# Gathering and turning the rows of two experts at once in a two-network fp32 kernel

## The reference, cut to what matters

```python
def expert_choice_moe(x, w_router, b_router, w_gate, w_up, w_down):
    b, s, d = x.shape
    cap = CAPACITY_FACTOR * s // N_EXPERTS            # 2 * 512 // 16 = 64 rows for each of 16 experts
    logits = jnp.einsum('bsd,de->bse', x, w_router).astype(jnp.float32) + b_router.astype(jnp.float32)
    aff = jax.nn.softmax(logits, axis=-1)
    gate, idx = lax.top_k(aff.transpose(0, 2, 1), cap)
    bidx = jnp.arange(b)[:, None, None]
    xs = x[bidx, idx]                                 # (b, 16, 64, 1024): the gather
    hid = jax.nn.silu(jnp.einsum('becd,edf->becf', xs, w_gate)) * jnp.einsum('becd,edf->becf', xs, w_up)
    ys = jnp.einsum('becf,efd->becd', hid, w_down) * gate[..., None].astype(x.dtype)
    return jnp.zeros_like(x).at[bidx, idx].add(ys)
```

## Time and profile before

| | |
|---|---|
| median of three runs | 2621.09 us |
| profiled execution, own time | 2624.85 us |
| its span, mean granted TensorE clock | 2622.9 us, 0.986 |
| TensorE busy (weight loads beside it) | 2505.8 us, 96% (1522.2 us) |
| VectorE, ScalarE, GpSimd busy | 1161.0, 476.1, 156.3 us |
| DMA, whole span | 601.78 MB, mean 229 GB/s |
| MoE stages | from about 1369 to 1840 us, and from about 2150 to the end |

### The profile page before, as it was taken

The page is one execution under the profiler, slowest core; times in us unless marked ns, Lnnn a source line. Parts: engine busy times, 40 slices in busy tenths (PEclk is TensorE's granted clock), DMA queues, the critical chain, the costliest instruction groups (busy, mean ns, idle before and its releaser), DMA issues.

```text
span 2622.9 us, 26789 instructions
## 1 busy us (share of the span) xinstructions
PE 2505.8 (96%) x10897; PEld 1522.2 (58%) x10897; DVE 1161.0 (44%) x2000; ACT 476.1 (18%) x1000; POOL 156.3 (6%) x265
## 2 busy tenths in 40 slices
PE   7999999999999999999999998889999999998898
PEld 4448888888888888556653333333556553333333
DVE  4774898655755644334641221112335641211112
ACT  2242121002222001234610000000224510000000
POOL 1140111000000000001200000000001000000000
PEclk9999999999999999999999999999999999999999
DMA  8642876451434225221259999999320359999998
GB/s 327 223 128 66 278 233 194 136 142 37 137 119 129 65 65 172 85 91 38 91 198 391 402 404 410 412 419 418 130 97 33 124 187 402 412 403 412 410 419 340
DMA packets 182794, 601.78 MB, mean 229 GB/s; under 512 B 9009, under 2 KB 123377, under 8 KB 157073
## 3 DMA queue, kind: packets, MB, share of 16 engines
q1 hardware_dynamic: 164544, 544.59, 54.7%
q0 software_dynamic: 16832, 51.22, 6.0%
q10 hardware_dynamic: 1296, 4.25, 0.4%
HBM read 593.74 MB, written 6.29 MB: 229 GB/s over the span
## 4 chain that ended last, share of the span: by engine, by line
PE 71%; DMA 18%; DVE 6%; ACT 1%; SPq 1%; issue 1%; another core or an unknown queue 0%; DVEq 0%; ACTq 0%
DMA arena<-in_w_down 17%; PE ps L2025 11%; PE ps L2583 7%; PE ps L2150 7%; PE ps L2613 6%; PE ps L2036 5%; PE ps L2262 5%; PE ps L2498 4%; PE ps L1996 3%; PE ps L2256 3%; PE ps L1945 2%; PE ps L2061 2%; PE ps L2276 2%; PE ps L2626 2%; PE ps L1920 1%; PE ps L2433 1%
## 5 line engine op out<-in xcount | busy, mean ns | idle before, releaser
L2583 PE MATMUL ps<-arena 128*64 128x512 f32 x2048 | 455.9, 599 | 20.3 <-DMA arena<-in_w_up 18.1
L2583 PEld LDWEIGHTS ps<-arena 128*64 128x64 f32 x2048 | 148.2, 138 | 311.8 <-issue 267.8
L2025 PE MATMUL ps<-arena 128*128 128x256 f32 x1280 | 277.9, 380 | 2.0 <-issue 2.0
L2025 PEld LDWEIGHTS ps<-arena 128*128 128x128 f32 x1280 | 242.9, 190 | 35.6 <-issue 3.4
L2613 PE MATMUL ps<-arena 128*64 128x512 f32 x896 | 211.1, 629 | 45.1 <-DMA arena<-in_w_down 43.7
L2150 PE MATMUL ps<-arena 128*128 128x256 f32 x896 | 193.8, 380 | 0.2 <-DVE arena L1453 0.2
L2150 PEld LDWEIGHTS ps<-arena 128*128 128x128 f32 x896 | 170.3, 190 | 23.4 <-issue 0.5
L2613 PEld LDWEIGHTS ps<-arena 128*64 128x64 f32 x896 | 72.3, 144 | 181.6 <-issue 179.9
L2036 PE MATMUL ps<-arena 128*128 128x256 f32 x672 | 146.3, 380 | 3.2 <-DVE arena L1266 1.7
L1804 DVE TENSOR_SCALAR arena<-ps,arena 128x512 f32<-128x512 f32 x32 | 22.7, 747 | 269.0 <-PE ps L2613 241.5
L2036 PEld LDWEIGHTS ps<-arena 128*128 128x128 f32 x672 | 127.6, 190 | 20.7 <-DVE arena L1274 2.0
(11 more groups left out here) (440 smaller groups left out, 3055.8 us busy)
## 6 DMA issues: line engine op xcount, KB each, us to landing
arena<-in_w_gate SPq DMA_DIRECT2D x64, 2048.0 KB, 49.1
arena<-in_w_up SPq DMA_DIRECT2D x64, 2048.0 KB, 41.9
arena<-in_w_down SPq DMA_DIRECT2D x56, 2048.0 KB, 41.7
arena<-in_ffn_w SPq DMA_DIRECT2D x24, 2048.0 KB, 9.8
arena<-in_w_mod POOLq DMA_DIRECT2D x80, 512.0 KB, 5.0
arena<-in_ffn_w SPq DMA_DIRECT2D x32, 1024.0 KB, 7.6
arena<-in_w_down SPq DMA_DIRECT2D x16, 1024.0 KB, 37.2
arena<-in_w_in SPq DMA_DIRECT2D x10, 1536.0 KB, 12.0
```

Source lines behind the costliest of these rows:

```text
L2025: ins = mm(ps[:, i % 6, 0:256], src[:, k, P * j:P * j + P], x[:, k, :], start=(k == 0), stop=(k == 3))
L2583: ins = mm(ps[CAP * half:CAP * half + CAP, bank, :], xsT[:, 4 * q + k, :], wv[:, k, 512 * half:512 * half + 512], start=(q == 0 and k == 0 ...
```

## The change

From the second pair of experts on, the rows of both experts come by one gather of 128 rows, over all 128 partitions. It is issued when the rows of the pair before are turned, in both rounds. The pair's rows are then turned in two rounds of four 128 x 128 transposes through PSUM bank 4; round 0 follows the products of the odd expert before, round 1 the first scatter behind it. TensorE's round 1 waits for VectorE's multiply of round 0. After even experts other than the first nothing is turned. Experts 0 and 1 are fetched and turned as before, except that VectorE's multiply is two operations of half the width. The turned rows of a pair take 1024 columns: `xsT` is now two tensors, one of them in the memory of the small tensors of the first block, which become parts of one tensor `first`. A copy of the index columns for pairs, `get_p`, is added on VectorE, and GpSimd waits for it.

```diff
--- before.py
+++ after.py
@@ -109,12 +109,13 @@
         ident, sel = const[:, C_ID:C_ID + P], const[0:8 * RPB_H, C_SEL:C_SEL + 8 * RPB_H]
         tbl = sb("tbl", [8 * RPB_H, 2, NA_HEADS, 40])
         ones = sb("ones", [P, P])
-        vrow = sb("vrow", [P, 2, P])
-        vA = sb("vA", [P, P])
-        vB = sb("vB", [P, B_ROWS])
+        first = sb("first", [P, 720])
+        vrow = first[:, 0:256].rearrange("p (i n) -> p i n", i=2)
+        vA = first[:, 256:384]
+        vB = first[:, 384:384 + B_ROWS]
         v2 = sb("v2", [P, DEPTH * VROWS])
-        modc = sb("modc", [P, 96])
-        small = sb("small", [P, 16, 8])
+        modc = first[:, 496:592]
+        small = first[:, 592:720].rearrange("p (i n) -> p i n", i=16)
         qkg = sb("qkg", [P, 2, DEPTH, QK])
         wr = sb("wr", [P, DEPTH, KC, EXPERTS])
         br = sb("br", [P, DEPTH, EXPERTS])
@@ -222,10 +223,13 @@
         get_i = at(38344, 16).bitcast(U32)
         idx_t = at(38360, 32, "p (i t) -> p i t", t=TC)
         iota = at(37952, P)
+        get_p = at(38392, 8).bitcast(U32)
         get_c = [sb(f"get_c{i}", [CAP, 1], U32) for i in range(2)]
+        get_pc = sb("get_pc", [P, 1], U32)
         oh = at(36928, 512)
-        xg = [at(38400, 1024)[CAP * i:CAP * i + CAP, :] for i in range(2)]
-        xsT = at(39424, 512, "p (k n) -> p k n", k=KC)
+        xg_pair = at(38400, 1024)
+        xg = [xg_pair[CAP * i:CAP * i + CAP, :] for i in range(2)]
+        xsT = [v.rearrange("p (k n) -> p k n", k=4) for v in (at(39424, 512), first[:, 0:512])]
         hid = at(39936, 512)
         hT2 = [at(lo, 512, "p (k n) -> p k n", k=4) for lo in (40448, 37440)]
         ye = [at(lo, 512) for lo in (40960, 49664)]
@@ -1757,6 +1761,7 @@
                 V.tensor_copy(get_i[0:CAP], idx_m).then_inc(sm["idx_cols"], 1)
                 dve.wait_ge(sm["top_ps"], 4 * l + 4)
                 V.tensor_copy(gate_t, ps[:, 6, 80:88])
+                V.tensor_copy(get_p, ps[:, 6, 88:96])
                 for t in range(TC):
                     ins = V.tensor_scalar(idx_t[:, :, t], ps[:, 6, 88:96], float(-P * t), None, add)
                 ins.then_inc(sm["idx_cols"], 1)
@@ -1765,8 +1770,16 @@
                 def gathered(e):
 
                     dve.wait_ge(sm["xst_ps"], 16 * l + e + 1)
-                    V.tensor_tensor(xsT, ps[:, 4, :].rearrange("p (k n) -> p k n", k=KC),
-                                    gperm[:, l, :].unsqueeze(2).to_broadcast([P, KC, CAP]), mul).then_inc(sm["xs_ready"], 1)
+                    for q in range(2):
+                        ins = V.tensor_tensor(xsT[q][:, :, CAP * e:CAP * e + CAP], ps[:, 4, 256 * q:256 * q + 256].rearrange("p (k n) -> p k n", k=4),
+                                              gperm[:, l, 4 * q:4 * q + 4].unsqueeze(2).to_broadcast([P, 4, CAP]), mul)
+                    ins.then_inc(sm["xs_ready"], 1)
+
+                def gathered_pair(i, q):
+
+                    dve.wait_ge(sm["xst_ps"], 16 * l + 2 * i + q + 1)
+                    V.tensor_tensor(xsT[q], ps[:, 4, :].rearrange("p (k n) -> p k n", k=4),
+                                    gperm[:, l, 4 * q:4 * q + 4].unsqueeze(2).to_broadcast([P, 4, P]), mul).then_inc(sm["xs_ready"], 1)
 
                 def scattered(i, t):
 
@@ -1785,10 +1798,15 @@
                     chain(V.scalar_tensor_tensor(hid, hid, 1.0, ps[:, 0, :], add, mul))
                     dve.wait_ge(*part_used(l, e, 3))
                     V.scalar_tensor_tensor(hid, hid, 0.5, ps[:, 1, :], mul, mul).then_inc(sm["hid_done"], 1)
-                    if e + 1 < EXPERTS:
-                        gathered(e + 1)
+                    if e == 0:
+                        gathered(1)
+                    elif par and e + 1 < EXPERTS:
+                        gathered_pair(i + 1, 0)
                     if i:
                         scattered(i - 1, 2 * par)
+                    if par and e + 1 < EXPERTS:
+                        gathered_pair(i + 1, 1)
+                    if i:
                         scattered(i - 1, 2 * par + 1)
                     if par == 0:
                         continue
@@ -2558,14 +2576,25 @@
 
                 def gathered(e):
 
-                    b = e % 2
-                    pe.wait_ge(got[b], 16 * (l * 8 + e // 2 + 1))
+                    pe.wait_ge(got[e], 16 * ((8 - 7 * e) * l + 1))
                     if e:
-                        pe.wait_ge(sm["ht_copied"], 16 * l + e - 1)
+                        pe.wait_ge(sm["ht_copied"], 16 * l)
                     for k in range(KC):
                         q, kk = divmod(k, 4)
-                        src = xg[b][:, 512 * q:512 * q + 512].rearrange("c (p k) -> c k p", k=4)[:, kk, :]
-                        ins = tr(ps[:, 4, CAP * k:CAP * k + CAP], src, ident[CAP * b:CAP * b + CAP, CAP * b:CAP * b + CAP])
+                        src = xg[e][:, 512 * q:512 * q + 512].rearrange("c (p k) -> c k p", k=4)[:, kk, :]
+                        ins = tr(ps[:, 4, CAP * k:CAP * k + CAP], src, ident[CAP * e:CAP * e + CAP, CAP * e:CAP * e + CAP])
+                    ins.then_inc(sm["xst_ps"], 1)
+
+                def gathered_pair(i, q):
+
+                    if q == 0:
+                        pe.wait_ge(got[0], 16 * (8 * l + i + 1))
+                        pe.wait_ge(sm["ht_copied"], 16 * l + 2 * i - 1)
+                    else:
+                        pe.wait_ge(sm["xs_ready"], 16 * l + 2 * i + 1)
+                    for kk in range(4):
+                        src = xg_pair[:, 512 * q:512 * q + 512].rearrange("c (p k) -> c k p", k=4)[:, kk, :]
+                        ins = tr(ps[:, 4, P * kk:P * kk + P], src, ident)
                     ins.then_inc(sm["xst_ps"], 1)
 
                 def piece(e, part):
@@ -2580,7 +2609,7 @@
                         wv, used = piece(e, part + q)
                         for k in range(4):
                             for half in range(2):
-                                ins = mm(ps[CAP * half:CAP * half + CAP, bank, :], xsT[:, 4 * q + k, :], wv[:, k, 512 * half:512 * half + 512],
+                                ins = mm(ps[CAP * half:CAP * half + CAP, bank, :], xsT[q][:, k, CAP * (e % 2):CAP * (e % 2) + CAP], wv[:, k, 512 * half:512 * half + 512],
                                          start=(q == 0 and k == 0), stop=(q == 1 and k == 3))
                         ins.then_inc(used, 1)
 
@@ -2629,21 +2658,25 @@
                 for e in range(EXPERTS):
                     i, par = divmod(e, 2)
                     n = 16 * l + e
-                    pe.wait_ge(sm["xs_ready"], n + 1)
+                    pe.wait_ge(sm["xs_ready"], 16 * l + (2 * i + 2 if i else e + 1))
                     inner(e, 0, 0)
                     if par == 0 and i:
                         pe.wait_ge(sm["ye_done"], 16 * l + 2 * i)
                     inner(e, 1, 2)
-                    if e + 1 < EXPERTS:
-                        gathered(e + 1)
+                    if e == 0:
+                        gathered(1)
+                    elif par and e + 1 < EXPERTS:
+                        gathered_pair(i + 1, 0)
                     if i:
                         pe.wait_ge(sm["oh_ready"], 8 * l + i)
                         scattered(i - 1, 2 * par)
                         if par == 0:
                             scattered(i - 1, 1)
+                    if par and e + 1 < EXPERTS:
+                        gathered_pair(i + 1, 1)
                     pe.wait_ge(sm["hid_done"], n + 1)
                     if e + 1 < EXPERTS:
-                        pe.wait_ge(sm["xs_ready"], n + 2)
+                        pe.wait_ge(sm["xs_ready"], 16 * l + (2 * (i + par) + 2 if e else 2))
                     for c in range(4):
                         ins = tr(ps[:, 4, P * c:P * c + P], hid.rearrange("p (n k) -> p k n", k=4)[:, c, :], ident)
                     ins.then_inc(sm["ht_ps"], 1)
@@ -2761,20 +2794,27 @@
 
                 def gather(e):
 
-                    b = e % 2
                     if e:
-                        G.tensor_copy(get_c[b][:, :], get_i[0:CAP, e:e + 1]).then_inc(sm["col_set"], 1)
-                        pool.wait_ge(sm["col_set"], 15 * l + e + 1)
-                    G.indirect_dma_start(out=xg[b], out_offset=None, in_=xn_dram,
-                                         in_offset=bass.IndirectOffsetOnAxis(ap=get_c[b][:, 0:1], axis=0)).then_inc(got[b], 16)
+                        G.tensor_copy(get_c[1][:, :], get_i[0:CAP, 1:2]).then_inc(sm["col_set"], 1)
+                        pool.wait_ge(sm["col_set"], 8 * l + 2)
+                    G.indirect_dma_start(out=xg[e], out_offset=None, in_=xn_dram,
+                                         in_offset=bass.IndirectOffsetOnAxis(ap=get_c[e][:, 0:1], axis=0)).then_inc(got[e], 16)
+
+                def gather_pair(i):
+
+                    G.tensor_copy(get_pc[:, :], get_p[:, i:i + 1]).then_inc(sm["col_set"], 1)
+                    pool.wait_ge(sm["col_set"], 8 * l + i + 2)
```

(9 more changed lines are left out.)

## The result

The changed kernel takes 2587.97 us (median of 4 runs, 2584.14 to 2589.86) against 2621.15 (2620.12 to 2622.59): 33.2 us less, ratio 0.987, 95% interval 0.986 to 0.988. The profiled execution took 2584.14 us with a span of 2582.3. The forecast was 2597 in 2586 to 2625, faster with 0.61.

A forecast was written before the change was run, and what follows sets the result against it. MoE stages were taken as bound by the weight DMA stream; dips -32.4 plus 7.0 left (-25.4), bytes +0.6 and head +0.3 gave -24.5: 2600.4 us profiled, 2597 as median, range 2586 to 2625.

The forecast's parts named there:

- The bound: MoE stages: from load 11 on, weight transfers set the end; TensorE work saved is worth nothing, DMA time itself.
- gather 2's bytes moved later: Layer 0: gather 2's rows, free before, now come inside the first pair gather in the full stretch, +0.6 us.
- The dips: MoE weight stream: the rate falls around each 64-row gather; 27 dips of 1.2 us, 32.4 us in the old kernel.
- What is left of a dip at full width: MoE weight stream: each 128-row pair gather still costs 0.5 us, 14 of them 7.0 us.
- head: Start of each MoE stage: two narrow multiplies behind gather 0 delay load 11 by 0.15 us, +0.3 over two layers.
- this very case: Landing in one half of the partitions causes the dips: 2597 us, own range 2588 to 2606, chance 0.52.
- the signs: Rate from 1400 to 1800 us rises from 411 to about 420 GB/s; each layer's stage ends about 12 us sooner.
- Turning: TensorE: even expert's gap -1.1 us, odd one's +1.3, per pair +0.2; no effect on the end.
- The doubtful place: First pair: buffers released at 1421.6 us, before loads under way run out at 1422.9; holds by little over 1 us.
- By rows: Rival for the MoE gathers: a dip's cost goes by rows, 2.4 us per 128-row gather; +2.1, 2623 us, chance 0.30.
- By transfer: Rival for the MoE gathers: each transfer costs one dip of 1.2 us whatever its width; -14.7, 2606 us, chance 0.10.
- Late pair gather: Rival: the first pair gather lands after 19.2 us, too late, and TensorE stalls; 2632 us, chance 0.08.

The follow-up runs named there:

- e10: Changed kernel with eight 64-row transposes per even expert put back as work without use (pairs 1 to 7); 2590.5 us, ratio 0.988.
- e2: Changed kernel, but from the third pair on two 64-row gathers, one into each partition half, one behind the other's landing; 2619.6 us, ratio 1.000.
- e3: As e2, but both 64-row gathers land in partitions 32 to 95; 2586.8 us, ratio 0.987.
- e5: Changed kernel with each 128-row gather from the third pair on done twice, one behind the landing of the other; 2604.2 us, ratio 0.994.
- e7: As e2, but four 32-row gathers, one into each quarter of the partitions, one behind the other; 2618.1 us, ratio 0.999.

## Why the prediction was right

- *The bound.* That each MoE stage ends with its weight stream, and that DMA time alone counts there, held: e10 (transposes back) moves the sum from load 11 on by 0.3 us, and e2 (new turning, old gathers) is back at the kernel before. There 893.9, 3 dips fewer (-3.8) and gather 2's bytes moved later (+0.6) make 890.7; 891.8 was measured.
- *The dips, 32.4 us.* Right in place, cause and size: 1.16 to 1.26 us each (e2 against e3) for the 1.2 taken, 27 x 1.26 = 34.0. The lower bound, 1.07, came from setting 411 against the 424 GB/s of a stretch without gathers; the changed kernel runs at 427 with its gathers, and (427 - 411)/427 x 400/12 = 1.25.
- *What is left of a dip at full width, 7.0 us.* The mis-sized term: 14 x 0.2 = 2.8 by the stages of e5, 0.6 by its rate. I took the price of a mix with stores out of all partitions; the loads of the earlier trace rows at 0.04 per transfer were the nearer kind, being loads into all partitions.
- *Bytes moved later, +0.6, and head, +0.3.* Not measured apart. The two narrow multiplies end at 1370.93 after 1370.17, 0.76 us where one took 0.69: +0.07, not +0.15.
- *The sum.* From load 11 on: -34.0 + 0.6 and 2.8 or 0.6 for the full-width gathers, -30.6 or -32.8, against -32.6 measured. The clock at the head of layer 0 adds 2.7 in the profiled pair; the sum had left it out and only the range allowed for it. How often it falls in executions without a profile is not known, so how much of the 33.2 us between the medians it is stays open. Predicted was -24.5.
- *How near.* The measured 2588 lies 9 us under the forecast and at the edge of the 2588 to 2606 given to this very case: the mechanism is right, the full-width gather was taken too dear, and with the dips slightly too cheap both errors point the same way; nothing cancelled. Of the signs, the rate rose to 427 GB/s for about 420, and the stages of layers 0 and 1 became 18.4 and 17.1 us shorter for about 12. (The lower end of the range adds up to 2585.3 by its own terms, and 14 x 0.04 is 0.6, not 0.7; neither changes the reading.)
- *Turning.* Odd experts' gap between products grew from 5.2 to 6.3 us and the first one's from 3.46 to 4.57, +1.1 each (predicted +1.3); even experts' shrank from 5.2 to 4.1, as predicted; no effect on the end. The doubtful place held: 429 GB/s from 1415 to 1420 and 1.01 busy. The outer product released its first buffers at 1413.5, 38.5 us behind load 11, and eight loads with one pair gather last about 41.
- *The rivals.* By rows: needed no gain; e2 and e3 move the same rows and differ by 33 us. By transfer: refuted by e3 and e7. Late pair gather: it landed after 12.6 us, and its first use came 1401.51 - 1386.84 = 14.7 us behind its issue, so it was in time by 2.1; in layer 1 after 11.3, with the same 14.7; later ones of layer 0 after 10.8 to 12.3.

The rule of the Trainium skill's SBUF — State Buffer, "Door 1: The DMA port swizzle", that 64 adjacent partitions from 0 or 64 reach 8 of 16 ports, while 32 to 95 reach all of them, agrees with every target tried: the halves and the quarters slow (1.26 us, and 0.62 for 32 rows), the middle, the alternate and the full width not. The traces do not show ports; they show partitions, and the price of 1.2 to 1.4 us for 256 KB beside a full weight stream.

## What to carry to other kernels

Where a stage is bound by a weight stream, look at the rate in short stretches around every small transfer, not at its bytes: a transfer of 256 KB (0.6 us) cost 1.3 us more because its 64 partitions lay in one half. Let small transfers land in partitions of both halves evenly (all 128, the middle 64, every other one), even at the price of more work on an engine that waits anyway. To decide on such a cause, keep number, size and waits of the transfers and change only where they land; and before a price is read from two profiles, look whether the clock fell at some head in one of them.

## What the runs showed of the hardware that was not expected

- A transfer into partitions of one half slows the core's whole DMA traffic, from 427 to between 305 and 330 GB/s, for about 5 of the 9.6 us to its landing (before, e2). It costs as much whether indirect (1.26 us) or plain (1.22), from GpSimd's queue or ScalarE's (1.26), and by the row as much with 32 rows at a time as with 64.
- Two such transfers into opposite halves, issued 1.4 us apart on one queue, do not cover each other: ten microseconds at 305 GB/s.
- Beside the stream a 64-row gather into one half landed after 9.6 us, one into the middle after 8.3 (e3), one of 128 rows after 11.4 (medians).
